# Projection slices spread through an RWKV-7 stage: the next head group's r, k, v inside the present group's inversion and chain, and the attention's first five projections between the steps of the samples' RWKV

## The chip, the core and the metric

The kernel runs on one core of one Trainium2 chip. The metric is the device time of one execution in microseconds (us), lower is better. The core has five engines that run side by side and meet at semaphores: TensorE (PE, matmuls; PEld is its weight load), VectorE (DVE), ScalarE (ACT), GpSimd (POOL) and SyncE (SP, which here only starts transfers). TensorE's clock is granted at one of two levels, 1.2 and 2.4 GHz; the profile gives it as 0.5 and 1.0.

## What is computed

One inference step of one decoder layer for 512 prompt tokens and 8 samples of 8 tokens (576 token columns in all), float32:

```python
x = x + 0.5 * SwiGLU(RMSNorm(x))                      # FFN 1
h = RMSNorm(x); P = h @ w_in                          # 1024 -> 4608 q,k,v | 1792 RWKV | 2048 gates
A = dilated sliding-window attention, 3 groups, QK-norm + ALiBi
u = p_shift + mu * (prev - p_shift)                   # token shift, gives r, k, v and the lora inputs
S = S * w_t - sk * (kk_t * a_t) + v_t * k_t ; o_t = S r_t     # RWKV-7 state, per head
o_rwkv = (layernorm(o) * gain + bias + bonus) * g
x = x + w_out( sigmoid(gA) * (A @ wa) + sigmoid(gR) * (R @ wr) )
x = x + 0.5 * SwiGLU(RMSNorm(x))                      # FFN 2
```

## The kernel before

**Units and slices.** Every projection is made in units: one unit is 128 output columns of a weight, over all 576 tokens, in three passes (high part of the weight by high and low part of the activation, low part by high part), each over eight tiles of the contraction. `unit_slice` (L333) issues one tile of the three passes, six matmuls of 128x128 by 288 columns: a slice. A unit is eight slices (KD = 8). Its weights come by one SP transfer into `w_raw` (`load_unit`, L309), are rounded by ACT into `w_hi` (`split_hi`, L315), and POOL subtracts to get `w_lo` (`split_lo`, L320). There are two buffers of each (even and odd units): a buffer's next weights are split after the unit before has been consumed, and the low part is what `unit_wait` on PE asks for, with the evacuation of the unit's PSUM banks. Units have a fixed order over the whole kernel, written out by hand on all engines and in the list `mids` on the host.

**Stages.** FFN 1; the prompt's RWKV (`rwkv_pe`, `rwkv_act`, `rwkv_dve`); a barrier; the samples' RWKV (`rwsam_*`); the output norm and gate of both (`rwout_*`); a barrier; attention (`att_*`); merge; FFN 2. A barrier is an order of PE, ACT and DVE alone (`barrier`, L351).

**The prompt's RWKV.** Two units for the lora inputs, then four head groups `ct` (two heads each). A head group starts with three units r, k, v for itself, each made at one go (`unit`); ACT copies each out of PSUM (`take`, L926), keeps the last token of each sequence (L929) and splits the weights two units on; DVE mixes it with the token before (`mix`, L1036 to L1041). Then come the lora matmuls (L722), the norm of kk (L730), transposes (L739), the bonus (L746), two products and five levels of a blockwise triangular inversion (L774; DVE's part L1104 to L1133, ACT's L989 and L995), three products, MV, XTK and W1 (L837, L845, L853), the transition matrices (L862), a chain of eight chunk states (L881, DVE L1156), and the output (L909, L916; DVE `UU` L1162; ACT L1014). Between these steps PE runs `fill(n)`: n slices of the head group's four gate units, 32 slices in all, whose results ACT stores to memory (`gate_out`, L954 and L957). `FILL` (line 83) says how many slices stand where. On ACT and DVE two head groups are one body of a loop of two.

**The samples' RWKV and the output.** Steps of 8 to 64 small matmuls with one DVE or ACT operation between them, no projection at all: transposes L1201, inversion L1183, the states (L1233 and L1248, 64x64 by 8 columns), the state updates (`SPREAD`, L1256 and L1257; DVE L1348), then per head group mean, variance and gate (L1375, L1383, L1390) with nine DVE operations (L1427 to L1440).

**Attention.** Four head groups with nine units each. The last four units of a head group are its own; the first five (AHEAD = 5) are made as slices in the head group before, and those of the first head group at one go at the start of the stage (`fill(AHEAD * KD, 0)`, 40 slices), with ACT's copies in front of everything else it does there. SP issues the mask and the weights of units 4 to 6 after barrier 3.

Of the kernel before, what the change touches and what calls it, by code (L numbers as in the profile page):

```python
# [23 lines left out]
ALU = mybir.AluOpType  # L24
# [7 lines left out]
NT = SEQ + NS  # L32
# [50 lines left out]
FILL = {"norm": 5, "tokens": (10, 1, 0, 0), "bonus": 0, "level": (1, 1, 1, 1, 0), "mv": 2, "xk": 2, "chunk": (1, 1, 1, 1, 1, 1, 1, 1)}  # L83
# [103 lines left out]
def build(nc, t):  # L187
# [11 lines left out]
    with ctx:  # L199
# [37 lines left out]
        beside_x.close()  # L237
        with ExitStack() as c:
# [7 lines left out]
            FM = sb(c, "fm", [128, 5, NT])  # L246
            KA, BH, KH, RH, UV = (FM[:, i] for i in range(5))
            TOK = sb(c, "tok", [128, 4, 4, 128])
            MV, W1 = sb(c, "mv", [128, 4, 128]), sb(c, "w1", [128, 4, 128])
            XK, UU = sb(c, "xk", [128, 512]), sb(c, "uu", [128, 4, 128])  # L250
            ST, XTK, GG = sb(c, "st", [128, NCH + 1, DH]), sb(c, "xtk", [128, 4, 128]), sb(c, "gg", [128, 2, 4, 128])
# [7 lines left out]
        with ExitStack() as c:  # L259
            QKV = sb(c, "qkv", [128, 3, 3, NT])  # L260
# [418 lines left out]
        def rw_units(i):  # L679

            return [(P_CT + 7 * i[0] + (7 * i[1] + n) // 2, (7 * i[1] + n) % 2, n) for n in range(3)]

        def gate_units(i):

            return [(P_CT + 7 * i[0] + (7 * i[1] + n) // 2, (7 * i[1] + n) % 2) for n in range(3, 7)]
# [7 lines left out]
        def rwkv_pe(pe):  # L693
            unit(pe, P_RW, 0, ready=("h_ready", 8, 0))
            unit(pe, P_RW, 1)
            pe.wait_ge(sem("lora_in_ready"), 2)
            for cc in range(2):
                for c2 in range(2):
                    ct = 2 * cc + c2
                    for P, q, n in rw_units((cc, c2)):  # L700
                        unit(pe, P, q)
                    filled = 0

                    def fill(slices):

                        nonlocal filled
                        for _ in range(slices):
                            P, q = gate_units((cc, c2))[filled // KD]
                            k = filled % KD
                            if k == 0:  # L710
                                unit_wait(pe, P, q)
                            last = unit_slice(q, h_hi, h_lo, k, k, KD, 2 * q)
                            if k == KD - 1:
                                last.then_inc(unit_done, 1)
                            filled += 1


# [8 lines left out]
                    fill(FILL["norm"])  # L726
# [1590 lines left out]
```

## Time and profile before

| | us |
|---|---|
| median of three runs (lowest, highest) | 1984.37 (1977.75, 1984.44) |
| the profiled execution, its own time | 1983.89 |
| its span, first to last instruction | 1982.1 |
| PE busy in the span | 1829.9 |
| DVE, ACT, POOL busy | 759.3, 627.3, 530.8 |
| prompt's RWKV, from its third unit to its last matmul | 492.7 to 906.9 |
| samples' RWKV and output, with both barriers | 906.9 to 1027.9 |
| the attention's first five units | 1027.9 to 1061.5 |

Times in a view are counted from the span's start. Busy time of PE is the union of its matmuls' durations, which overlap; the time of a run of like matmuls is read from start to start. In a row of a timeline the bracket gives the idle time ahead of it and what ended it.

### The profile page before, as it was taken

The page shows a single profiled execution, that of the slowest core. Times are in us where ns is not written, and L with a number is a line of the kernel's source. Part 1 is how long each engine was busy: PE and PEld are TensorE (multiplying, and loading weights), DVE is VectorE, ACT ScalarE, POOL GpSimd, SP SyncE. Part 2 cuts the span into 40 slices and gives each one's busy share as a digit, 9 for nine tenths or more (in the row PEclk, how much of TensorE's full clock was granted, in tenths as well). Part 3 has the DMA queues.
Part 4 walks back from the last instruction along what each step waited for, and adds up shares of the span by engine and source line. Part 5 has one row for each costly group of instructions (what it writes and reads, how often), then busy time and mean ns, then how long its engine had stood idle before and what let it go on. Part 6 is the DMA issues. An engine that isn't in the chain of part 4 may idle for free.

```text
span 1982.1 us, 41842 instructions
## 1 busy us (share of the span) xinstructions
PE 1829.9 (92%) x17032; PEld 1724.1 (87%) x17032; DVE 759.3 (38%) x1120; ACT 627.3 (32%) x828; POOL 530.8 (27%) x206
## 2 busy tenths in 40 slices
PE   7999999995898999887869999999899999999998
PEld 6999999994788888876549898988699999999998
DVE  4332033215535444452353454535456533113320
ACT  4332122223414141312024343434343433123321
POOL 2443344431203030300002121212033344334432
PEclk9999999998999999997569999999799999999999
DMA  4334333423404040411005444444453333333342
GB/s 152 118 116 138 103 114 119 135 96 111 157 29 144 25 175 30 152 40 68 17 25 182 163 161 163 168 160 168 178 192 106 117 126 116 128 112 122 113 143 110
DMA packets 52167, 237.47 MB, mean 120 GB/s; under 512 B 6992, under 2 KB 7632, under 8 KB 50512
## 3 DMA queue, kind: packets, MB, share of 16 engines
q1 hardware_dynamic: 44176, 219.40, 32.3%
q10 hardware_dynamic: 7872, 16.37, 2.2%
q8 instruction: 89, 1.46, 0.3%
q14 instruction: 30, 0.25, 0.0%
HBM read 217.98 MB, written 71.76 MB: 146 GB/s over the span
## 4 chain that ended last, share of the span: by engine, by line
issue 82%; POOL 13%; PE 4%; POOLq 1%; ACT 0%; ACTq 0%
POOL w_lo L320 13%; PE ps L333 4%; POOLq L627 0%; POOLq L319 0%; POOLq L2131 0%; POOLq L630 0%; ACT w_hi L315 0%; POOLq L320 0%; POOLq L626 0%; ACTq L314 0%; POOLq L2301 0%
## 5 line engine op out<-in xcount | busy, mean ns | idle before, releaser
L320 POOL TENSOR_TENSOR w_lo<-w_raw,w_hi 128x1024 fp32r<-128x1024 f32 (+1 forms) x202 | 530.6, 2627 | 1429.6 <-ACT w_hi L315 1429.6
L333 PE MATMUL ps<-h_hi,w_hi 128*128 128x288 f32 x2464 | 552.1, 306 | 40.6 <-POOL w_lo L320 14.0
L333 PE MATMUL ps<-h_lo,w_hi 128*128 128x288 f32 x2464 | 531.3, 298 | 0.0
L333 PE MATMUL ps<-h_hi,w_lo 128*128 128x288 f32 x2464 | 531.1, 297 | 0.0
L333 PEld LDWEIGHTS ps<-h_hi,w_hi 128*128 128x128 f32 x2464 | 400.0, 191 | 60.9 <-POOL w_lo L320 16.3
L333 PEld LDWEIGHTS ps<-h_lo,w_hi 128*128 128x128 f32 x2464 | 401.2, 191 | 0.0
L333 PEld LDWEIGHTS ps<-h_hi,w_lo 128*128 128x128 f32 x2464 | 400.4, 191 | 0.0
L315 ACT ACTIVATE w_hi<-w_raw 128x1024 fp32r<-128x1024 f32 (+1 forms) x204 | 226.3, 1109 | 432.8 <-PE ps L333 415.5
L333 PE MATMUL ps<-g_hi,w_hi 128*128 128x288 f32 x704 | 151.5, 297 | 0.1
L333 PE MATMUL ps<-g_lo,w_hi 128*128 128x288 f32 x704 | 151.3, 297 | 0.0
L333 PE MATMUL ps<-g_hi,w_lo 128*128 128x288 f32 x704 | 151.2, 297 | 0.0
L589 DVE SCALAR_TENSOR_TENSOR gt<-ps,nry 128x576 f32<-128x576 f32 x44 | 33.4, 758 | 241.1 <-PE ps L333 241.1
L333 PEld LDWEIGHTS ps<-g_hi,w_hi 128*128 128x128 f32 x704 | 113.7, 189 | 1.1 <-POOL w_lo L320 1.1
L602 DVE SCALAR_TENSOR_TENSOR x<-ps,x 128x576 f32 (+1 forms) x32 | 24.2, 758 | 235.9 <-PE ps L333 235.9
L333 PEld LDWEIGHTS ps<-g_hi,w_lo 128*128 128x128 f32 x704 | 113.8, 189 | 0.0
L333 PEld LDWEIGHTS ps<-g_lo,w_hi 128*128 128x128 f32 x704 | 113.8, 189 | 0.0
L595 DVE TENSOR_TENSOR g_lo<-gt,g_hi 128x576 f32 x44 | 87.4, 1986 | 42.4 <-ACT g_hi L555 42.4
L550 ACT ACTIVATE sg<-sg 128x576 f32<-128x576 f32 x44 | 30.2, 686 | 158.2 <-DVE sg L586 158.2
L586 DVE SCALAR_TENSOR_TENSOR sg<-ps,nry 128x576 f32<-128x576 f32 x44 | 33.4, 758 | 88.2 <-PE ps L333 87.5
L1734 ACT ACTIVATE qkv<-ps 128x576 f32<-128x576 f32 x36 | 23.4, 651 | 127.1 <-PE ps L333 127.1
L774 PE MATMUL ps<-xt,lmask 64*64 64x64 f32 x640 | 29.6, 237 | 14.7 <-DVE lmask L1110 8.2
L550 ACT ACT_TABLE_LOAD x30 | 38.5, 1283 | 13.0 <-issue 13.0
(365 smaller groups left out, 2023.1 us busy)
## 6 DMA issues: line engine op xcount, KB each, us to landing
w_raw<-in_w SPq DMA_DIRECT2D x172, 512.0 KB, 3.5
w_raw<-in_w SPq DMA_DIRECT2D x32, 704.0 KB, 4.0
kv<-in_kc SPq DMA_DIRECT2D x32, 576.0 KB, 5.9
kv<-in_vc SPq DMA_DIRECT2D x32, 576.0 KB, 7.3
cache_out<-in_cache SPq DMA_DIRECT2D x28, 576.0 KB
gates<-gate_out ACTq DMA_DIRECT2D x16, 288.0 KB, 2.1
gate_in<-gates SPq DMA_DIRECT2D x8, 576.0 KB, 5.0
cache_out<-in_cache SPq DMA_DIRECT2D x8, 480.0 KB
```

Source lines behind the costliest of these rows:

```text
L315: nc.scalar.activation(w_hi[par_][:, 0:words], w_raw[par_][:, 0:words], ACT.Copy).then_inc(hi_done, 1)
L320: nc.gpsimd.tensor_tensor(w_lo[par_][:, 0:words], w_raw[par_][:, 0:words], w_hi[par_][:, 0:words].bitcast(F32), ALU.subtract).then_inc(lo_ ...
L333: last = nc.tensor.matmul(ps[:, b + c, 0:HC], w[par_][:, wk], a[:, k, c * HC:(c + 1) * HC], start=(first and k == 0), stop=(end and k == n ...
L550: nc.scalar.activation(sg[:, :], sg[:, :], ACT.Silu).then_inc(sem("silu_done"), 1)
L586: nc.vector.scalar_tensor_tensor(two(sg[:, :]), bank2(0), back(0), two(nry[:, :]), ALU.mult, ALU.mult).then_inc(evac[0], 1)
L589: nc.vector.scalar_tensor_tensor(two(gt[:, :]), bank2(2), back(0), two(nry[:, :]), ALU.mult, ALU.mult).then_inc(evac[1], 1)
L595: nc.vector.tensor_tensor(g_lo[:, j, :], gt[:, :], g_hi[:, j, :].bitcast(F32), ALU.subtract).then_inc(sem("g_ready"), 1)
L602: nc.vector.scalar_tensor_tensor(two(x[:, k, :]), bank2(2 * q), 0.5, two(x[:, k, :]), ALU.mult, ALU.add)\
L774: last = nc.tensor.matmul(ps[rows_of(e), 4 + (2 * n + h) % 4, 64 * T:64 * T + 64], lhs(T, e), rhs(T, e), start=True, stop=True)
L1734: nc.scalar.activation(two(QKV[:, g, kind, :]), bank2(b), ACT.Copy).then_inc(evac[q], 1)
```

## The change

What it does, in parts:

1. **Order of units** in the prompt's RWKV (`RW_UNITS`, and `mids` on the host): lora 2, r, k, v of head group 0, then for each `ct` gates 0 to 2, r, k, v of `ct + 1`, gate 3.
2. **PE**: only the five first units are made at one go. The other 25 (200 slices) come through `fill`, with counts that add up to 56 a head group (53 up to the end of the first one, 35 left for the last one). New places: ahead of the products, at the fifth level, and in the tail.
3. **ACT**: `gate_out` and `take` stand at new places in the queue: gate 3 of the group before after the square of kk, gates 0 and 1 ahead of the copies of the transposes, gate 2 ahead of LR, r after the levels, k after W1, v ahead of the copy of the output. The waits for stored gates at a head group's end are gone. PR is chosen by the count of mixes.
4. **DVE**: the mixes of `ct + 1` stand after the products and at the end of the chain. The loops of ACT and DVE are written out. DVE waits for `x_kept` before the first mixes of r, k, v.
5. **Memory**: QKV of the attention and part of the RWKV's tiles (FM, MV, UU, XTK, ST) lie over the same space outside the stages' own, so that the attention's raw projections can be written during the samples' RWKV.
6. **Samples' RWKV and output**: 40 slices of the attention's first five units in 16 fills of 2, 3 or 6, PSUM banks 0 and 1 for them; the stage's own banks are moved up, the gate of the output has one pair of banks in place of two (so that it waits for the DVE's last operation of the head group before), ACT takes the raw projections and splits the next weights between its steps. Variance goes before the next mean on PE.
7. **Output on DVE**: three operations (L1436, L1437, L1438) become two.
8. **Attention**: its 40 slices at the start are gone, with ACT's five copies and splits. One memset (L1840) is gone, the scaled masks (L1888) are made after `spread` in each head group, SP loads weights 4 to 7 ahead of barrier 3 and the masks behind the first three key transfers.

```diff
-FILL = {"norm": 5, "tokens": (10, 1, 0, 0), "bonus": 0, "level": (1, 1, 1, 1, 0), "mv": 2, "xk": 2, "chunk": (1, 1, 1, 1, 1, 1, 1, 1)}
+FILL = {"norm": 9, "tokens": (11, 1, 1, 0), "bonus": 2, "products": 3, "level": (3, 2, 2, 2, 2), "mv": 3, "xk": 2,
+        "chunk": (1, 1, 1, 1, 1, 1, 1, 1), "tail": (3, 2)}
+RW_UNITS = [("lora", 0, 0), ("lora", 0, 1)] + [("mix", 0, n) for n in range(3)]
+for _ct in range(CT):
+    RW_UNITS += [("gate", _ct, n) for n in range(3)] + [("mix", _ct + 1, n) for n in range(3) if _ct + 1 < CT] + [("gate", _ct, 3)]
...
             for cc in range(2):
                 for c2 in range(2):
                     ct = 2 * cc + c2
-                    for P, q, n in rw_units((cc, c2)):
-                        unit(pe, P, q)
...
-                    fill(FILL["norm"])
+                    fill(FILL["norm"] if ct else KD - 2)
...
+                    fill(FILL["products"])
...
+                    fill(FILL["tail"][0])
...
+                    fill(FILL["tail"][1])
...
                     act.wait_ge(sem("kkr_ready"), ct + 1)
                     nc.scalar.activation(TT[:, :], KA, ACT.Square).then_inc(sem("kk_sq"), 1)
                     act.drain()
+                    if ct:
+                        gate_out(ct - 1, 3)
...
-                    gate_out(0)
+                    gate_out(ct, 0)
+                    gate_out(ct, 1)
                     for a in range(2):
...
-                    gate_out(1)
...
+                    gate_out(ct, 2)
...
+                    if ct + 1 < CT:
+                        take("mix", ct + 1, 0)
+                    else:
+                        gate_out(ct, 3)
                     act.wait_ge(sem("mv_done"), ct + 1)
...
+                    if ct + 1 < CT:
+                        take("mix", ct + 1, 1)
                     for half in range(2):
                         act.wait_ge(sem("xk_done"), 2 * ct + half + 1)
...
-                    gate_out(2)
...
+                    if ct + 1 < CT:
+                        take("mix", ct + 1, 2)
                     act.wait_ge(sem("o_done"), ct + 1)
...
-                    gate_out(3)
-                    for q in range(2):
-                        act.wait_ge(sem("gate_stored%d" % q), 16 * (2 * ct + 2))
-                    act.wait_ge(sem("wkvp_stored"), 16 * (ct + 1))
...
-            scores(0, 0, 1)
-            scores(2, 1, 0)
+            scores(2, 0, 1)
+            fill(2)
+            pe.wait_ge(sem("s_tok_a"), 2)
+            scores(4, 1, 0)
+            fill(6)
             pe.wait_ge(sem("s_inv"), 1)
             pe.wait_ge(sem("s_tok_d"), 2)
             heads(6, mm(SLM), mm(SXT))
+            fill(2)
             pe.wait_ge(sem("s_act"), 2)
             heads(7, mm(SZZ), mm(SXX))
             heads(4, mm(SXX), mm(SZZ))
+            fill(3)
             pe.wait_ge(sem("s_inv"), 2)
             heads(6, mm(SLM), mm(SXT))
+            fill(3)
...
                 nc.tensor.matmul(o, TOS[1][:, hc(ct, h)], SPREAD[h][0], start=True, stop=False)
                 nc.tensor.matmul(o, TOS[2][:, hc(ct, h)], SPREAD[h][1], start=False, stop=True).then_inc(sem("s_dstate"), 1)
+                if h:
+                    fill(2)
...
             mean(0)
             gate(0)
-            for ct in range(CT):
+            mean(1)
+            fill(2)
+            var(0)
+            fill(2)
+            for ct in range(1, CT):
+                var(ct)
                 if ct + 1 < CT:
                     mean(ct + 1)
-                var(ct)
-                if ct + 1 < CT:
-                    gate(ct + 1)
+                    fill(2)
+                gate(ct)
...
-                own(V.tensor_tensor(FT[:, :], FO[ct % 2][:, :], FY[ct % 2][:, :], ALU.mult))
-                own(V.tensor_scalar(FT[:, :], FT[:, :], P1("lng", ct), P1("lnb", ct), ALU.mult, ALU.add))
-                own(V.tensor_tensor(FT[:, :], FT[:, :], BN[:, ct, :], ALU.add))
+                own(V.scalar_tensor_tensor(FT[:, :], FO[ct % 2][:, :], P1("lng", ct), FY[ct % 2][:, :], ALU.mult, ALU.mult))
+                own(V.scalar_tensor_tensor(FT[:, :], FT[:, :], P1("lnb", ct), BN[:, ct, :], ALU.add, ALU.add))
...
-                if hp == 0:
-                    fill(AHEAD * KD, 0)
-                    filled = 0
                 own_slices(0, 0, 2)
                 norm(0)
```

## Rows read from the trace of the kernel before

**Rows 1.** The page, busy time of PE and its weight loads.

```profile
PE 1829.9 (92%) x17032; PEld 1724.1 (87%) x17032; DVE 759.3 (38%) x1120; ACT 627.3 (32%) x828; POOL 530.8 (27%) x206
```

**Rows 2.** Busy time by stage: length, then each engine, then clock and DMA.

```profile
492.70:595.90 103.20, 92.69 (x1259) 84.98 (x1259) 45.86 (x87) 29.01 (x47) 14.96 (x6) 0.96 0.26 94
...
801.10:906.90 105.80, 93.36 (x1259) 85.37 (x1258) 49.52 (x87) 29.92 (x49) 17.81 (x7) 0.95 0.24 85
906.90:912.60 5.70, 0.00 (x0) 0.00 (x0) 0.00 (x0) 2.19 (x3) 2.34 (x1) 0.74 0.13 52
912.60:939.30 26.70, 19.63 (x224) 17.91 (x225) 9.64 (x15) 4.82 (x7) 0.00 (x0) 0.61 0.24 82
939.30:951.70 12.40, 11.18 (x136) 10.56 (x133) 0.68 (x1) 0.97 (x2) 0.00 (x0) 0.54 0.00 1
951.70:966.90 15.20, 15.14 (x160) 15.04 (x160) 0.00 (x0) 0.00 (x0) 0.00 (x0) 0.50 0.01 1
966.90:989.50 22.60, 20.20 (x32) 5.91 (x32) 14.84 (x23) 0.38 (x1) 0.00 (x0) 0.50 0.09 35
989.50:1027.90 38.40, 19.35 (x48) 11.93 (x48) 24.91 (x34) 8.82 (x13) 0.00 (x0) 0.63 0.02 8
1027.90:1061.50 33.60, 33.60 (x236) 33.60 (x237) 5.27 (x8) 8.11 (x9) 9.57 (x4) 0.93 0.25 78
```

**Rows 3.** PE's waits from 492 to 907: us in total, times, longest.

```profile
PE ps L739 <- DVE fm L1065: 8.4, 4, 2.2
PE ps L774 <- DVE lmask L1110: 8.2, 8, 1.5
...
PE ps L333 <- POOL w_lo L320: 5.0, 2, 3.1
...
PE ps L739 <- DVE fm L1072: 0.6, 3, 0.2
```

**Rows 4.** PE's waits from 907 to 1028.

```profile
PE ps L1383 <- DVE tmp L366: 5.5, 3, 2.7
PE ps L1390 <- DVE o_rw L1440: 4.8, 2, 2.5
PE ps L1183 <- DVE lmask L1312: 3.4, 1, 3.4
...
PE ps L1183 <- DVE lmask L1318: 2.0, 1, 2.0
...
PE ps L1183 <- ACT zz L1262: 1.4, 2, 0.7
...
PE ps L1183 <- ACT xx L1262: 0.2, 1, 0.2
```

**Rows 5.** Timeline of PE: start, duration; slices and heads at either clock.

```profile
493.87 0.68 PE L333 MATMUL ps<-h_hi,w_lo 128*128 128x288 f32 x2
...
495.31 0.68 PE L333 MATMUL ps<-h_hi,w_lo 128*128 128x288 f32 x2
...
920.90 1.96 PE L1183 MATMUL ps<-xt,lmask 64*64 64x64 f32 x16 [3.43 <-DVE lmask L1312]
...
938.35 1.14 PE L1183 MATMUL ps<-xx,xt 64*64 64x64 f32 x16 [0.21 <-ACT xx L1262]
...
1058.06 0.43 PE L333 MATMUL ps<-h_hi,w_hi 128*128 128x288 f32 x2
...
1058.87 0.42 PE L333 MATMUL ps<-h_hi,w_hi 128*128 128x288 f32 x2
```

**Rows 6.** DVE's L1063 and L1061 (one form), from source and timeline.

```profile
L1063 DVE SCALAR_TENSOR_TENSOR tmp<-fm,sw x4: 2811/2820/2821, 527.8 to 839.3; 128x576 f32<-128x576 f32 x4
...
833.67 0.76 DVE L1061 SCALAR_TENSOR_TENSOR u_k<-fm,u_k 128x576 f32<-128x576 f32 x1
```

**Rows 7.** PE in the state updates: length, busy, clock, DMA.

```profile
972.00:988.00 16.00, 16.00 (x28) 0.50 0.08 33
```

**Rows 8.** Timeline of DVE, the operation that falls away.

```profile
1002.58 0.58 DVE L1437 TENSOR_SCALAR tmp<-tmp,par 128x576 f32<-128x576 f32 x1
```

More of the change, by code:

```diff
@@ L677, in build, with rw_unit @@
         IN_BANK = (7, 4)
[L679 to L685, printed above, removed]
+        def rw_unit(kind, ct, n):
+            i = RW_UNITS.index((kind, ct, n))
+            return P_RW + i // 2, i % 2
         def rows_of(h):
@@ L696, in rwkv_pe, with fill @@
             pe.wait_ge(sem("lora_in_ready"), 2)
+            for n in range(3):
+                unit(pe, *rw_unit("mix", 0, n))
+            filled = 0
+            def fill(slices):
+                nonlocal filled
+                for _ in range(slices):
+                    i, k = 5 + filled // KD, filled % KD
+                    if i == len(RW_UNITS):
+                        return
+                    P, q = P_RW + i // 2, i % 2
+                    if k == 0:
+                        unit_wait(pe, P, q)
+                    last = unit_slice(q, h_hi, h_lo, k, k, KD, 2 * q)
+                    if k == KD - 1:
+                        last.then_inc(unit_done, 1)
+                    filled += 1
             for cc in range(2):
@@ L1178, in mc, with ahead_pe, fill, rwsam_pe @@
             return slice(256 * h + 64 * ct, 256 * h + 64 * ct + 64)
-        def rwsam_pe(pe):
+        def ahead_pe(pe, of, state):
+            def fill(slices):
+                if of == CT:
+                    return
+                for _ in range(slices):
+                    n, k = state[0] // KD, state[0] % KD
+                    P, q = at_unit(of, n)
+                    if k == 0:
+                        unit_wait(pe, P, q)
+                        if of or n:
+                            Pb, qb = at_unit(of, n - 1)
+                            pe.wait_ge(evac[qb], Pb + 1)
+                    last = unit_slice(q, h_hi, h_lo, k, k, KD, FBANK)
+                    if k == KD - 1:
+                        last.then_inc(unit_done, 1)
+                    state[0] += 1
+            return fill
+        def rwsam_pe(pe, fill):
             def heads(bank, lhs, rhs, where=mc):
@@ L1712, in att_pe @@
                     fill(5)
-                    assert hp + 1 == CT or filled == AHEAD * KD
+                    assert hp + 1 == CT or state[0] == AHEAD * KD
         def att_act(act):
@@ L1750, in guess @@
                     rsqrt_act(own, bank2(NORM_BANK[i]), ary[i % 2], 3)
-                if hp == 0:
-                    for n in range(AHEAD):
-                        take(0, n)
                 square_of(0)
@@ L1898, in att_dve @@
                     spread()
+                    if hp == 0:
+                        dve.wait_ge(sem("mask_loaded"), 16)
+                    for h in range(2):
+                        V.tensor_scalar(MSC[:, h, :], MSK[:, 0:512], P1("slp", 2 * hp + h), None, ALU.mult)
+                    dve.drain()
                     apply(4)
@@ L2067, in _ @@
             barrier(pe, 2)
-            rwsam_pe(pe)
-            rwout_pe(pe)
+            first = [0]
+            fill = ahead_pe(pe, 0, first)
+            rwsam_pe(pe, fill)
+            rwout_pe(pe, fill)
+            assert first[0] == AHEAD * KD
             barrier(pe, 3)
@@ L2097, in _ @@
             act.wait_ge(sem("shift_stored"), 16)
+            for i in range(2):
+                act.wait_ge(sem("gate_stored%d" % i), 16 * 2 * CT)
             act.wait_ge(sem("x_kept"), 16)
```

227 lines of the change are left out of this document (115 added, 112 removed).

## The prediction

> **What bounds the kernel now.** I read the page first: PE is busy for 1829.9 of 1982.1 us [rows 1]. That is a union of overlapping matmuls, so at best 152 us of the span are open, and only PE's order of work can give time back. Next I cut the span at the code's stages [rows 2]. The reader should see three kinds of stretch. A head group of the prompt's RWKV takes 103 to 106 us, of which PE is busy for some 93, near full clock. From 912.6 to 1027.9 there is no projection: PE's clock is 0.50 to 0.63 and between the barriers only the small steps run. From 1027.9 to 1061.5 it is the reverse: PE works without a gap, DVE and ACT are nearly idle. Last I asked for PE's waits in the first two kinds [rows 3, 4]: each is a wait of a few us at most for one DVE, ACT or POOL operation. PE's order bounds all of it; the waits are the only room.
>
> **Price of a slice.** Two like passes of neighbouring slices start 495.31 - 493.87 = 1.44 us apart at the half clock and 1058.87 - 1058.06 = 0.81 at the full one [rows 5]; over a whole unit the full pitch is 0.80. So a slice is 0.80 or 1.44 us. The change keeps their number. What it can gain is waits filled, and clock; what it can lose is new waits.
>
> **A, the prompt's RWKV (492.7 to 906.9).** PE's waits there, without the one ahead of 492.75 that stays, are twelve rows of the view with a sum of 42.9 us [rows 3]. Twenty-four slices of each of head groups 1 to 3, now made at one go, move into the steps, and fills grow exactly where the waits are: 9 for 5 ahead of the norm, 13 for 11 in the transposes, 5 new ones ahead of bonus and products (4.0 us, more than the longest of these waits), 11 for 4 in the levels. Waits with no slices ahead of them (L845, L746, and three of the transposes' short ones) make 5.3 us. So 37.6 can go; 5.0 of it are the stands for `w_lo` [rows 3], where split and unit followed each other too closely at the old head group's start.
>
> Three things come back. First, the last head group has 35 slices left in place of 56: from the fifth level on its steps run bare. At most 0.80 is uncovered at each of the eleven or so places, 8.8 in all, at least nothing; I take 5, as a chain step's own DVE latency is about half of what its slice covered. Second, ACT: five copies that PE waits for (TOK, LR, MV, XK, the output) now stand behind a copy and a split of about 2 us. I followed each: for MV and the output the unit is ready early and the step itself is slower than ACT; for TOK and LR the margins are under 1 us. Third, POOL beside DVE. L1063, with two inputs in SBUF, takes 2.82 us in all four head groups, L1061 of the same form 0.76 [rows 6]; each L1063 starts while POOL is in a `w_lo`. So an exposed meeting costs 2.06 us. Before, POOL made none of a head group's splits between the first products and the chain's second half; now three to four of the seven splits fall there, onto the DVE operations after the first products, on the first mixes and, by `gate_out(ct, 1)` moved ahead, on BH and KH. Bounds: none exposed, 0; one at each of the five places in four head groups, 20 x 2.06 = 41. The nearest rows are the two margins under 1 us, so I take 2.65 us a head group, 10.6: one meeting and half a microsecond of ACT. A = -(37.6 - 5 - 10.6) = **-22**, from -32.6 to +8.4.
>
> The GPSIMD Engine Reference of the Trainium skill (Specifications) says that GpSimd shares its SBUF interfaces with VectorE and that they contend when a VectorE instruction has two SBUF inputs. The trace agrees (2.82 against 0.76), and this speaks against the change: taken for every split that now falls into the inversion it would give the upper bound, not the value taken.
>
> Unrolled loops on ACT and DVE, and the wait for `x_kept`, I cost at nothing: PE's unit 3 covers the latter; if that transfer came later, head group 0 would start late by as much.
>
> **B, the end of the stage.** The 5.70 us between the last matmul and the first of the samples hold only ACT's last copies, gate 3's store and a wait for it, with PE at nothing [rows 2]. The store moves ahead; the state's own store remains. Between -4 and 0, I take **-2**.
>
> **C, samples' RWKV and output (912.6 to 1027.9): 40 slices, 31.9 us at the full clock, 57.6 at the half one.** Step by step:
> - 912.6 to 939.3, 20 slices, 15.9 us (28.8). They stand ahead of waits of 3.4 + 2.0 + 1.4 + 0.2 = 7.0 [rows 4]. Eight heads' matmuls take 1.96 us at the half clock and 1.14 near the full one [rows 5]; with dense slices between I expect the full clock for most, and five such steps gain 4: +5. Bounds +4 and +21.8.
> - 939.3 to 966.9: 4 slices. Their own clock will be low (64x8 matmuls run at 0.50 to 0.54 through 27 us with PE busy [rows 2]), 5.8 us less 1.3 of waits, less 1 for the first steps at a better clock: +3.5. Bounds +1, +4.5.
> - 966.9 to 989.5, the state updates: 8 slices. PE is busy 20.20 of 22.60 at 0.50, DVE 14.84 [rows 2]. At the half clock PE is the bound and 8 x 1.44 = 11.5 add up, less 1.6 that cover the last update's DVE part: +10. At the full clock PE's part halves and DVE is the bound: 0. I take +4.
> - 989.5 to 1027.9: 8 slices, ahead of waits of 5.5 + 4.8 = 10.3 [rows 4]. DVE sets the pace (24.91 busy, each step following on its own or ACT's last). It loses L1437's 0.58 four times [rows 8], -2.4 with the issue. The first fill stands ahead of `var(0)`, which PE would reach at once: +1.5. The gate's single bank pair makes its matmuls wait, but DVE needs them only some 6 us later. -1; bounds -2.4 and +2.
>
> C = +5 + 3.5 + 4 - 1 = +11.5, taken as **+12**, from +3 to +38.
>
> **D, attention.** The 33.6 us of 1027.9 to 1061.5 are 40 slices and nothing beside them that something waits for [rows 2]: ACT's five copies and splits go with them. 33.6 - 40 x 0.80 = 1.7 is the start at the half clock, which the next units now pay. **-31.9**. What is late next: the first norm waits for ACT's squares, which now start behind a table load, some 2 us, as PE's two slices do; the key transfers start with the stage, about where they stood against the unit they precede; the masks come behind three of them, used only after `spread`. I price these at 0. The scaled masks moved on DVE: 0, PE has slices beside them.
>
> **Sum.** -22 - 2 + 12 - 31.9 = -43.9. The profiled execution took 1983.89, 0.5 under the median of the runs, so both stand for the same level: 1983.9 - 43.9 = **1940**.
>
> **Rivals.**
> 1. *All of it at the full clock.* If the slices lift the clock through the samples' stage, C is +3 and the time 1931. For it: stretches dense with slices run at 0.93 to 0.96 [rows 2]. Against it: 16 us of state updates with PE busy for 16.00 ran at 0.50 [rows 7]. The page TensorE: Matmul & The Clock Gate of the Trainium skill (Part 1) has the clock rise with sustained PE busyness; the trace disagrees here, as these matmuls were busy throughout and the clock stayed low. By the page's rule the present clock would be no guide, and this rival would be the forecast. Chance 0.15.
> 2. *The half clock stays through the samples' stage.* C is +38, the time 1966. For it: every row from 940 to 989.5. Against: slices at 1.44 us each make PE denser than anything in it now. Chance 0.10.
> 3. *The prompt's RWKV gains nothing*: waits filled come back behind ACT and POOL. A = 0, 1962. For it: 2.82 against 0.76 and the thin margins. Against: the waits are many and short. Chance 0.12.
> 4. *Slower: the ACT queue.* One mechanism: in the prompt's RWKV, ACT stands for the last slice of a unit while the copy that PE needs queues behind it, so that PE makes slices in place of steps and then stands. Five places in four head groups; without A the change gives -21.9, so at 1.1 us each they eat it, and at 1.6 (+0.5%) decide. The most is about 2 us of copy and split and 2.06 of POOL, 4.1 us each: 82, or 2044. Against it: three of the places have slack of several us. Chance 0.04.
> 5. *No change*, by half of rivals 3 and 2 together with a late weight transfer: within 0.5%, 0.05.
>
> The forecast keeps 0.54. Its own range is 1932 to 1954. The range for 8 in 10 takes in rival 1 and 3 and most of the way to 2: 1922 to 1964. 0.5% is 10 us, about what a measurement of this kernel can tell from no change. Faster by more: 0.54 + 0.15 + 0.10 + 0.12 = 0.91; within: 0.05; slower: 0.04.
>
> **What would show it.** After the change head groups 1 and 2 should take about 97 us, the last one under 90, the first about 112 (it has 75 slices in place of 56). PE's waits there should add up to less than 20, those for `w_lo` to none. Between the last prompt matmul and the attention's own first unit there should be some 131 us, with all 40 slices inside, and granted clocks well above 0.6 before the 64x8 matmuls. The attention should begin with `own_slices`. DVE operations of two SBUF inputs that take 2 us and more inside the inversion would prove the POOL term; PE waits for `zz`, `lraw` or `tok` the ACT one. The prediction is wrong if the samples' stage grows by more than 25 us, or if slices and steps in a head group add up to the old 104.

## Result and the profile after

The changed kernel takes 1916.67 us (median of 4 runs, 1911.29 to 1919.15) against 1982.28 (4 runs, 1977.75 to 1984.44) of the kernel before, in turns on the same chip: ratio 0.967, 95% interval 0.964 to 0.970. It is faster, and by more than forecast: 1916.67 lies under the range of 1922 to 1964. Its profiled execution took 1916.84, with a span of 1915.0, so 67.1 less than the one of before.

I cut both spans at the same instructions. The boundaries are: PE's third unit of the prompt's RWKV, ACT's last copy of the output, the first transposes of the samples, the attention's first unit, and the merge's first matmul.

| us | before | after | difference | predicted |
|---|---|---|---|---|
| start to the prompt's third unit | 492.8 | 490.7 | -2.1 | 0 |
| A, prompt's RWKV | 414.2 | 382.8 | -31.4 | -22 |
| B, its end to the samples' first step | 5.6 | 1.3 | -4.3 | -2 |
| C, samples' RWKV and output | 115.3 | 114.2 | -1.1 | +12 |
| D, attention | 403.7 | 376.3 | -27.4 | -31.9 |
| merge and FFN 2 | 550.5 | 549.7 | -0.8 | 0 |
| sum | 1982.1 | 1915.0 | -67.1 | -43.9 |

Over all profiles below, the first row lies between 490.7 and 493.8 whatever the kernel, so its 2.1 is no part of the change. A and C are the two terms that missed, by 9.4 and 13.1.

The page's first line after the change, against [rows 1]:

```profile
PE 1796.3 (94%) x17032; PEld 1703.2 (89%) x17032; DVE 777.8 (41%) x1115; ACT 623.4 (33%) x825; POOL 534.4 (28%) x206
```

The same 17032 matmuls took 33.6 us less. The slices are as many as before, so the shorter union of busy time comes from matmuls that ran faster (the mean clock over the span rose from 0.951 to 0.969) or that overlap more; how much of it is the clock is worked out for the prompt's stage under E6. Busy time by stage, with the columns of [rows 2]: head groups 0, 2 and 3, the end, then the samples' stage up to the 64x8 matmuls, these up to the second group of them, up to the state updates, the state updates, the output.

```profile
490.70:603.80 113.10, 106.12 (x1373) 99.49 (x1373) 54.45 (x97) 32.25 (x54) 22.84 (x9) 0.97 0.33 118
698.80:792.70 93.90, 88.80 (x1259) 82.84 (x1259) 49.61 (x88) 29.92 (x49) 18.23 (x7) 0.98 0.35 127
792.70:873.50 80.80, 73.46 (x1145) 67.56 (x1144) 44.67 (x78) 25.79 (x43) 13.44 (x5) 0.98 0.24 79
873.50:874.80 1.30, 0.03 (x1) 0.03 (x2) 0.00 (x0) 0.57 (x2) 0.00 (x0) 1.00 0.00 0
874.80:904.30 29.50, 29.50 (x345) 27.63 (x346) 9.65 (x15) 8.24 (x11) 4.74 (x2) 1.00 0.23 75
904.30:918.70 14.40, 14.40 (x159) 14.05 (x156) 0.68 (x1) 0.97 (x2) 0.00 (x0) 0.64 0.01 1
918.70:931.80 13.10, 10.75 (x161) 10.64 (x160) 1.70 (x3) 2.09 (x3) 2.34 (x1) 0.71 0.13 41
931.80:953.00 21.20, 21.14 (x80) 11.73 (x80) 14.53 (x23) 0.00 (x0) 0.00 (x0) 0.78 0.10 38
953.00:989.00 36.00, 21.45 (x99) 16.04 (x97) 23.65 (x28) 12.27 (x17) 4.73 (x2) 0.86 0.07 23
```

The reader should compare the clocks with [rows 2]. The first 20 slices of the samples' stage and the steps between them run at 1.00 where the steps alone ran at 0.61: 29.5 us now hold 15.9 us of slices and take 2.8 us more than the 26.7 without (4.2 more than the 25.3 of E1 below, which has the change without these slices). Further on 0.64, 0.71, 0.78 and 0.86 stand where 0.50 to 0.63 stood.

The same in two rows of PE's timeline, after: the 64x8 matmuls of the second group, 16 of a head in 1.05 us (before 1.82).

```profile
918.99 1.05 PE L1298 MATMUL ps<-sv,tok 64*64 64x8 f32 x16
920.16 0.99 PE L1298 MATMUL ps<-sv,tok 64*64 64x8 f32 x15
```

PE's waits in the prompt's stage after, the largest of it (the 8.7 us stand ahead of the stage, as before):

```profile
PE ps L776 <- DVE lmask L1125: 12.2, 8, 1.6
PE ps L338 <- ACT u_g L958: 8.7, 1, 8.7
PE ps L741 <- DVE qkv L1087: 4.4, 3, 1.5
PE ps L741 <- DVE qkv L1083: 2.2, 1, 2.2
PE ps L848 <- DVE lmask L1157: 2.0, 4, 0.5
...
PE ps L338 <- POOL w_lo L325: 0.8, 1, 0.8
```

The stands ahead of the norm (tmp) and the bonus are gone, and of those for `w_lo` 0.8 is left; the first level's wait for `lmask` (8.2 in [rows 3]) has grown to 12.2. The sum is 23.4 us, against 42.9 before.

### The profile page after: what moved, and what is told of

Same layout as the page of the kernel before. It is cut to its first block, busy times and chain, and to the rows that moved or that the text cites. A ratio compares the mean times of both kernels' runs of the same rounds, so it can differ in the third digit from the quotient of the medians.

```text
span 1915.0 us, 41445 instructions
## 1 busy us (share of the span) xinstructions
PE 1796.3 (94%) x17032; PEld 1703.2 (89%) x17032; DVE 777.8 (41%) x1115; ACT 623.4 (33%) x825; POOL 534.4 (28%) x206
## 4 chain that ended last, share of the span: by engine, by line
issue 81%; POOL 14%; PE 4%; POOLq 1%; ACT 0%; ACTq 0%
POOL w_lo L325 14%; PE ps L338 4%; POOLq L632 0%; POOLq L324 0%; POOLq L2183 0%; POOLq L635 0%; ACT w_hi L320 0%; POOLq L325 0%; POOLq L631 0%; ACTq L319 0%; POOLq L2360 0%
## 5 line engine op out<-in xcount | busy, mean ns | idle before, releaser
L1004 ACT ACTIVATE zz<-ps 128x256 f32<-128x256 f32 x40 | 15.4, 384 | 91.9 <-PE ps L776 90.7
```

The source lines that it names most:

```text
L1004: nc.scalar.activation(ZZ[h][:, 0:256], ps[:, 4 + (2 * n + h) % 4, 0:256], ACT.Copy).then_inc(sem("mat_a%d" % h), 1)
```

## Experiments

Two theories went into them. Theory 1: slices between small steps lift TensorE's clock, so the steps themselves get shorter; that would explain C, and the part of A that filled waits can't. Theory 2, the rival: the slices cost what they cost, and the gain comes from other parts (the shorter output on DVE, the new order, fewer waits).

All profiles, cut as above:

| us | A: head groups 0, 1, 2, 3 | A | C | state updates to first mean | D |
|---|---|---|---|---|---|
| before | 103.3, 104.1, 101.1, 105.8 | 414.2 | 115.3 | 21.8 | 403.7 |
| changed | 113.1, 95.0, 93.9, 80.7 | 382.8 | 114.2 | 21.2 | 376.3 |
| changed, again | 114.6, 92.6, 96.1, 83.2 | 386.5 | 122.4 | 28.4 | 372.9 |
| E1 prompt only | 114.8, 92.6, 94.4, 84.1 | 385.8 | 112.2 | 21.8 | 406.2 |
| E2 masks back | 115.0, 92.6, 93.4, 83.0 | 384.0 | 114.3 | 21.1 | 369.7 |
| E3 no late slices | 115.0, 92.5, 94.2, 81.9 | 383.6 | 118.1 | 21.1 | 371.6 |
| E4 gate 2 later | 112.7, 90.5, 90.5, 78.7 | 372.3 | 115.8 | 20.6 | 375.1 |
| E5 gate 1 later | 111.6, 92.2, 92.2, 80.4 | 376.5 | 116.1 | 20.4 | 374.1 |
| E6 all moves | 107.5, 88.8, 88.8, 76.9 | 361.9 | 114.2 | 21.1 | 369.7 |
| E6 again | 108.0, 88.8, 88.8, 77.0 | 362.5 | 116.1 | 20.4 | 367.7 |
| E7 three operations | 114.9, 92.6, 94.2, 81.8 | 383.4 | 125.9 | 28.1 | 374.3 |
| E8 slices ahead | 108.0, 88.8, 88.8, 77.0 | 362.5 | 114.4 | 16.8 | 367.7 |

### E1: the prompt's part alone

All 40 slices go back to the start of the attention, with ACT's copies and splits; everything else stays as changed.

```diff
-            rwsam_pe(pe, fill)
-            rwout_pe(pe, fill)
+            rwsam_pe(pe, lambda slices: None)
+            rwout_pe(pe, lambda slices: None)
...
+                if hp == 0:
+                    for n in range(AHEAD):
+                        P, q = at_unit(0, n)
+                        unit_wait(pe, P, q)
+                        for k in range(KD):
+                            last = unit_slice(q, h_hi, h_lo, k, k, KD, 2 * (n % 2))
+                        last.then_inc(unit_done, 1)
                 own_slices(0, 0, 2)
...
```

> The changed kernel with the 40 slices of the samples' RWKV and output taken out again and made at one go at the start of the attention, as before, with ACT's copies; the rest of the change stays. Theory 1 (the slices keep TensorE at 2.4 GHz in a stage that otherwise runs at 1.2, so they cost nothing): from the first transposes to the attention 111 to 113 us (115.3 before, less 2.4 for DVE's operation), granted clock again about 0.5 in the 64x8 matmuls and the state updates, attention's start again 33.6; in all the time rises by about 31 us over the changed kernel, to 1948. Rival (the recorded sum: slices cost 12 us net there): it rises by 20, to 1937.

Measured 1948.73 us (4 runs, 1948.25 to 1953.43) against 1982.04, ratio 0.984 (0.982 to 0.987), as theory 1 had it. So about half of the gain is the prompt's part and half the slices in the samples' stage. Windows of E1, cut like those of after (transposes, first 64x8 group, up to the state updates, state updates, output, and the five units at one go):

```profile
878.30:903.60 25.30, 18.19 (x224) 17.02 (x225) 9.65 (x15) 4.81 (x7) 0.00 (x0) 0.66 0.13 45
903.60:915.80 12.20, 10.99 (x135) 10.36 (x133) 0.68 (x1) 0.97 (x2) 0.00 (x0) 0.55 0.01 1
915.80:933.40 17.60, 15.16 (x161) 15.07 (x161) 1.71 (x3) 0.38 (x1) 0.00 (x0) 0.50 0.00 1
933.40:955.20 21.80, 20.20 (x33) 5.95 (x33) 14.51 (x22) 0.00 (x0) 0.00 (x0) 0.50 0.09 36
955.20:990.50 35.30, 19.39 (x49) 12.20 (x49) 21.69 (x28) 8.84 (x13) 0.00 (x0) 0.74 0.02 8
990.50:1024.00 33.50, 33.50 (x241) 33.50 (x242) 2.63 (x5) 8.08 (x9) 9.57 (x4) 0.95 0.18 55
```

Without slices the clock of the 64x8 matmuls and the updates is 0.50 to 0.55 again. The stage takes 112.2 us, so 40 slices, 31.9 us at the full clock, cost 2.0 in the first profile of the changed kernel (114.2) and give back 33.5 at the attention's start. By part, the changed kernel less E1: up to the 64x8 matmuls 29.5 - 25.3 = +4.2; up to the state updates 27.5 - 29.8 = -2.3; state updates -0.6; output +0.7. The other parts of the change in this stage are worth 115.3 - 112.2 = 3.1, of which 1.4 fall before the 64x8 matmuls (26.7 against 25.3, no slices in either) and 1.5 in the output. Theory 2 has those 3.1, theory 1 the rest. The 2.0 are those of one profile; the changed kernel's second profile, below, gives another figure.

### E3: no slices between the first 64x8 matmuls and the state updates

The last two fills of 2 are moved ahead of the first 64x8 matmuls, so that their number stays.

```diff
-            fill(2)
+            fill(4)
             pe.wait_ge(sem("s_dve"), 2)
...
-            fill(2)
+            fill(4)
             pe.wait_ge(sem("s_act"), 4)
...
-            fill(2)
             pe.wait_ge(sem("s_act"), 6)
...
-            fill(2)
             pe.wait_ge(sem("s_dve"), 6)
```

> The changed kernel with the two fills of 2 slices between the two groups of 64x8 matmuls moved ahead of the first group. Theory 1 (the slices matter for the clock of what follows them): the second group, 13.1 us, runs at 1.2 GHz again and takes about 15 us from its first matmul, the state updates start at 1.2 GHz, and the stage from the transposes to the attention grows by 2 to 4 us. Rival (the slices only fill waits of 1.3 us): the stage changes by less than 1.5 us, as the four slices are cheaper at the full clock.

Measured 1917.55 us (one run). The windows of E3 on both sides of the first 64x8 group, and up to the state updates:

```profile
878.60:911.50 32.90, 32.85 (x369) 31.00 (x370) 9.65 (x15) 8.25 (x11) 4.75 (x2) 1.00 0.21 67
911.50:922.20 10.70, 9.46 (x136) 8.84 (x134) 0.68 (x1) 2.66 (x4) 0.00 (x0) 0.65 0.01 2
922.20:939.70 17.50, 15.13 (x160) 15.03 (x160) 1.71 (x3) 0.41 (x2) 2.34 (x1) 0.50 0.10 31
```

The last row is the second 64x8 group: 17.5 us at 0.50 for the same steps that take 13.1 at 0.71 with four slices ahead of them. Where the four slices stand is nearly all one for themselves: 3.4 us more in the first part (32.9 against 29.5), 3.7 less in the second (10.7 against 14.4). But the steps behind lose 4.4, and the stage is 3.9 us longer. That is theory 1 at one place: the slices' own time is earned back by the steps behind them.

The 4.4 depend on the profile that E3 is held against. The three profiles without slices ahead of this group (before, E1, E3) all have 17.5 at 0.50. The eight with the changed kernel's fills have 13.0 to 13.2 in four (changed, changed again, E2, E6) and 15.3 to 15.7 in the other four. The row of E6's second profile:

```profile
899.90:915.40 15.50, 13.10 (x162) 13.00 (x161) 1.71 (x3) 2.09 (x3) 2.34 (x1) 0.58 0.11 35
```

So the four slices are worth 1.8 to 4.5 us behind them; the sign is certain, the size is not. The same holds for the stage: E3's 118.1 is 2.0 to 3.9 above the six profiles with these fills and fast updates (114.2 to 116.1).

### The changed kernel again, and E7: three operations in the output

The changed kernel, unedited; and the changed kernel with the three DVE operations of before:

```diff
-                own(V.scalar_tensor_tensor(FT[:, :], FO[ct % 2][:, :], P1("lng", ct), FY[ct % 2][:, :], ALU.mult, ALU.mult))
-                own(V.scalar_tensor_tensor(FT[:, :], FT[:, :], P1("lnb", ct), BN[:, ct, :], ALU.add, ALU.add))
+                own(V.tensor_tensor(FT[:, :], FO[ct % 2][:, :], FY[ct % 2][:, :], ALU.mult))
+                own(V.tensor_scalar(FT[:, :], FT[:, :], P1("lng", ct), P1("lnb", ct), ALU.mult, ALU.add))
+                own(V.tensor_tensor(FT[:, :], FT[:, :], BN[:, ct, :], ALU.add))
```

> The changed kernel once more, on the same chip as the version with three moves, for comparison: 1917, and within 3 us of it in each stage of the profile.

> The changed kernel with the output's three DVE operations per head group in place of two. Theory 1 (DVE sets the pace from the last state update to the attention): this stretch grows by 2.4 us, four times 0.6. Rival (ACT's guess or PE's new order sets it): by less than 1 us.

Measured: 1922.70 us for the changed kernel (5 runs, 1917.94 to 1927.83; ratio 0.969, 0.966 to 0.972), 1927.66 for E7 (one run). I had expected every stage of the changed kernel within 3 us of its first profile; A is 3.7 off and C 8.2. In both kernels the stretch from the first state update to the first mean takes 28 us where it takes 20 to 21 in the other profiles with these fills. The window of the changed kernel's second profile there:

```profile
936.60:965.00 28.40, 28.40 (x81) 15.55 (x82) 14.52 (x22) 0.00 (x0) 0.00 (x0) 0.50 0.07 28
```

PE is busy for all of 28.40 us, at 0.50; in the first profile the same instructions take 21.2 at 0.78 (above). The code is the same, so the clock there comes out one way or the other from run to run, and the 7.2 us between them are most of the 8.2 by which C differs between the two profiles. A single profile of this kernel therefore settles C to no better than that: by this one the 40 slices cost 122.4 - 112.2 = 10.2 us, not 2.0. E7 is best read against the second profile, which had the slow updates too: from the first mean to the attention it takes 38.2 us against 37.0, so the saved operation is worth 1.2 us, not the 2.4 that I took; E1, with no slices in either kernel, gives 36.8 - 35.3 = 1.5 for this part of the change. E7 is one run, and against the first profile (36.0) it would be 2.2, so the size is open between 1.2 and 2.2. The groups of DVE in the output show why, first of E7 (L1521 of the even head groups), then of the first profile after:

```profile
L1521 DVE TENSOR_TENSOR tmp<-exp_p,cumx 128x576 f32<-128x576 f32 x2 | 3.5, 1771 | 0.1
L1523 DVE TENSOR_TENSOR tmp<-tmp,bonus 128x576 f32<-128x576 f32 x4 | 3.0, 759 | 0.1
...
L1522 DVE TENSOR_SCALAR tmp<-tmp,par 128x576 f32<-128x576 f32 x4 | 2.3, 578 | 0.1
```

```profile
L1521 DVE SCALAR_TENSOR_TENSOR tmp<-exp_p,par,cumx 128x576 f32<-128x576 f32 x2 | 3.6, 1800 | 0.1
L1522 DVE SCALAR_TENSOR_TENSOR tmp<-tmp,par,bonus 128x576 f32<-128x576 f32 x4 | 3.3, 819 | 0.1
```

One operation of 0.578 is gone, and two of 0.759 have become 0.819: DVE has 0.46 less to do per head group, 1.8 in all. L1521 has a mean of 1800 because one of its two instances takes 2.78 beside a POOL split: head group 2's meets the split of the attention's weights, in E7 as well.

### E4 and E5: take POOL's splits off two DVE operations

What did A lose? The timeline of head group 2 after the change, first DVE, then POOL:

```profile
719.59 0.76 DVE L1085 TENSOR_TENSOR qkv<-u_k,exp_m 128x576 f32<-128x576 f32 x1
720.44 2.76 DVE L1087 TENSOR_TENSOR qkv<-u_r,exp_p 128x576 f32<-128x576 f32 x1
...
731.41 1.82 DVE L1121 TENSOR_TENSOR xx<-lraw,con 128x256 f32<-128x256 f32 x1 [0.82 <-ACT lraw L998]
733.26 0.42 DVE L1122 TENSOR_TENSOR xx<-xx,con 128x256 f32<-128x256 f32 x1
```

```profile
719.80 2.79 POOL L325 TENSOR_TENSOR w_lo<-w_raw,w_hi 128x1024 fp32r<-128x1024 f32 x1 [3.34 <-ACT w_hi L320]
730.56 2.38 POOL L325 TENSOR_TENSOR w_lo<-w_raw,w_hi 128x1024 fp32r<-128x1024 f32 x1 [7.97 <-ACT w_hi L320]
```

RH (L1087, the product whose transposes PE makes last) and the first product of the inversion behind ACT's copy (L1121) each start inside a split and end 0.61 and 0.29 us behind its end: 2.76 for 0.76 and 1.82 for 0.42. L1121 is also 0.82 late behind ACT's `lraw`, which stood behind the split's first half. Both operations stand on PE's path. So E4 makes gate 2's copy and split one step later on ACT, behind the first level's copy, and E5 gate 1's behind the copies of TOK:

```diff
-                    gate_out(ct, 2)
                     act.wait_ge(sem("x_kept"), 16)
...
+                        if lv == 0:
+                            gate_out(ct, 2)
```

```diff
                     gate_out(ct, 0)
-                    gate_out(ct, 1)
...
                         act.drain()
+                    gate_out(ct, 1)
```

> The changed kernel with ACT's copy of gate 2, its split and store moved behind the first level's copies in each head group. Theory 1 (ACT's queue, 0.8 us, and POOL's split beside the first DVE operation of the inversion, 1.4 us, hold up its start): the waits for lmask fall from 12.2 us to about 5, that DVE operation takes 0.43 us in place of up to 1.82, each head group gets 2 us shorter, the prompt's RWKV some 8 us. Rival (the two waits are the DVE chain itself, POOL only moves on to the next level): less than 2 us in all, with DVE operations of over 1.5 us in the levels.

> The changed kernel with ACT's copy of gate 1, its split and store moved behind the copies of the first two transposes, where it stood before. Theory 1 (POOL's split beside RH costs the last transposes their 1.47 us): RH takes 0.76 us in all head groups in place of 2.76, PE's wait for it goes, the prompt's RWKV gets 4 to 5 us shorter. Rival (PE is late elsewhere, as the copies come no earlier to it): less than 1.5 us.

Measured 1908.1 and 1911.15 us (one run each). Six profiles with A as changed have a mean of 384.4 (382.8 to 386.5); E4 has 372.3 and E5 376.5, so -12.1 and -7.9, and both lie clear of the six. The operation's row (count: shortest, median, longest in ns), in E4:

```profile
L1122 DVE TENSOR_TENSOR xx<-lraw,con x8: 424/425/426, 545.9 to 819.5; 128x256 f32<-128x256 f32 x8
```

and in the changed kernel, where it is 1822 at the most:

```profile
L1121 DVE TENSOR_TENSOR xx<-lraw,con x8: 425/1122/1822, 542.4 to 828.9; 128x256 f32<-128x256 f32 x8
```

PE's wait for the operations behind it, in E4:

```profile
PE ps L776 <- DVE lmask L1126: 4.0, 4, 1.0
```

The wait of 12.2 is 4.0, less than the 8.2 of before. In E5 RH takes 759 ns at the most and the waits at L741, 4.4 and 2.2 in the changed kernel, are 0.2. The mechanism is shown by E5: taking the meeting away takes the wait away. E4 takes away the meeting and ACT's 0.82 us together, so how the 8.2 divide between them is not shown. The GPSIMD Engine Reference of the Trainium skill (Specifications) has GpSimd and VectorE contend for the SBUF interfaces when a VectorE instruction reads two operands there; by that rule, the trace agrees.

But the stage gains more than the wait: 12.1 for 8.2, 7.9 for 6.4. The windows from the first product of head group 1 to the end of its inversion show where to look: before, changed, the changed kernel's second profile, E6.

```profile
642.00:671.00 29.00, 24.89 (x571) 22.72 (x572) 15.31 (x37) 4.60 (x12) 0.52 (x1) 0.88 0.15 44
```

```profile
633.75:666.80 33.05, 29.93 (x614) 27.95 (x614) 16.64 (x37) 7.63 (x17) 2.39 (x1) 0.90 0.09 30
```

```profile
636.30:666.90 30.60, 27.47 (x613) 25.38 (x613) 16.60 (x37) 7.58 (x17) 2.39 (x1) 1.00 0.10 32
```

```profile
629.20:657.50 28.30, 27.21 (x612) 25.19 (x612) 15.04 (x37) 7.41 (x17) 2.38 (x1) 1.00 0.21 71
```

In the first profile the clock falls within this stretch (0.90), in the second, with the same stands, it does not (1.00). So one head group decides nothing; all of them together do. I counted the stretch from the first product to the last matmul of the inversion in every head group. The seven profiles with the stands ahead of the first level (changed twice, E1, E2, E3, E5, E7) have 28 such stretches: the clock fell to 0.89 to 0.95 in 20 and stayed at 1.00 in 8. The four without (E4, E6 twice, E8) have 16, all at 1.00. In head groups 0 to 2 the stretch takes 28.0 us without the stands, 30.1 with them at 1.00, and 31.4 to 32.6 where the clock fell (three stretches, 30.9, 31.9 and 33.6, are left out: PE stood a further 0.5 to 1.6 us in them for no cause that the trace names). E4 and E5 tell the stands apart: E4 still has those at the transposes, and all four of its stretches are at 1.00; E5 has only those ahead of the first level, and all four are at 0.94 to 0.95. So a stand here costs its length, 2.1 us a head group, and in most cases 1.3 to 2.5 us more by the clock.

### E2 and E6: the masks at their old place, and all moves together

E2 puts DVE's scaled masks, for all head groups but the first, back behind the state's products at the end of the head group before. E6 is E2, E4 and E5 together.

```diff
+                    if hp:
+                        for h in range(2):
+                            V.tensor_scalar(MSC[:, h, :], MSK[:, 0:512], P1("slp", 2 * hp + h), None, ALU.mult)
+                        dve.drain()
                     v_place(1)
...
```

> The changed kernel with the scaled masks (two DVE operations of 0.88 us) made ahead of v_place again in head groups 1 to 3. Theory 1 (they now stand on the path from the norms to the first scores, 1.8 us each head group): the time falls by 5 us, to 1911, the attention from 376 to 371 us, and PE's waits for nmx and vsam shrink. Rival (hidden, as in the recorded prediction; the attention's extra comes from its start): no change, the attention stays at 376.

> The changed kernel with three moves together: masks back, gate 2 late, gate 1 late. Theory 1: the three add up, 5 + 8 + 5 = 18 us, to about 1899. Rival (each frees only what the next wait takes): 1908 to 1917.

> The version with all three moves once more, on the same chip as the version with two slices ahead of the state updates. Its time should be that measured for it before, 1896.6, within 6 us; head groups 361 to 363 us together, state updates 21 or 28 us.

Measured: E2 1914.96 us (1913.01 to 1916.72; ratio 0.966, 0.964 to 0.968), E6 1896.64 (5 runs, 1890.61 to 1899.27; ratio 0.956, 0.953 to 0.959) and once more 1893.28 (ratio 0.955, 0.953 to 0.957). By D, six profiles with the masks behind `spread` (without E1, which has five units more in D) have a mean of 374.1 (371.6 to 376.3), the four with them back 368.7 (367.7 to 369.7): the move that I priced at 0 costs 5.4 us. Half of it is idle time of PE in this stage, 18.9 to 20.9 us in the six and 16.9 to 17.5 in the four; the other half is busy time, where the two sets overlap, so its cause is not shown. PE's waits for the scores' scaling in the attention, changed, then E2:

```profile
PE ps L1661 <- DVE nmx L1956: 3.2, 5, 0.7
```

```profile
PE ps L1661 <- DVE nmx L1960: 1.3, 2, 0.7
```

Of the whole time E2 alone resolves nothing (1914.96 beside 1916.67 and 1922.70). E6 does: it beats both kernels, 20.0 and 23.4 us under the changed one's 1916.67, and 26.1 under the 1922.70 measured beside it. A is 361.9 and 362.5, so 22 us under 384.4, where E4 and E5 alone add up to 20.0. The prompt's stage as a whole, in windows of before, changed and E6:

```profile
492.70:906.90 414.20, 370.82 (x5032) 339.65 (x5032) 189.94 (x348) 120.10 (x195) 67.59 (x27) 0.96 0.26 93
```

```profile
490.70:873.50 382.80, 358.31 (x5032) 333.81 (x5032) 198.33 (x348) 117.88 (x195) 72.74 (x28) 0.97 0.29 103
```

```profile
493.50:855.40 361.90, 352.04 (x5032) 328.22 (x5032) 184.83 (x348) 117.77 (x194) 71.13 (x28) 0.99 0.31 109
```

The same 5032 matmuls. PE's idle time (length less busy) goes 43.4, 24.5, 9.9; its busy time 370.8, 358.3, 352.0, with the clock at 0.96, 0.97, 0.99. To three digits the clock is 0.958, 0.973 and 0.991. The stage's length times the share not granted, 17.4, 10.3 and 3.3 us, is an upper estimate of what the half clock cost, so the clock explains at most 7.1 of the 12.5 us of busy time that the changed kernel saves, and at most 14.1 of the 18.8 of E6. What the other 5 us or so are is not shown.

### E8: slices in the one wait that is left in the samples' stage

E6 with two slices ahead of the state updates, where PE waits 2.4 us for the first spread, and none behind the last update.

```diff
+            fill(2)
             for ct, h in HEADS:
...
-                if h:
+                if h and ct + 1 < CT:
                     fill(2)
```

> The version with all three moves (gate copies 1 and 2 later, scaled masks at their old place) and, in the samples' RWKV, two slices ahead of the state updates, where TensorE stands for some 2.4 us, and none after the last update. The slices stay 40. In the profiles so far the 64x64 matmuls by 512 columns of the updates ran either with the clock rising after the second update (about 21 us from the first of them to the first mean) or at half throughout (about 28 us) with the same code. If the clock hangs on how closely slices stand ahead of the updates, two slices in the wait bring the stretch to 18 to 20 us in the profile and to no 28; slices in the wait cost nothing, the two after the last update fall away: stage at 112 to 113 us, time 1893 to 1896, 0 to 4 under the version without. If it is chance that does not depend on the order, the time is that of the version without within 2 us, and the profile can show 28 again. If DVE sets the updates at the full clock, the stretch can't fall below about 17.

Measured 1895.78 us (5 runs, 1890.95 to 1901.81; ratio 0.957, 0.955 to 0.959), beside 1893.28 of E6 on the same chip: no gain. Windows of E8 from the second 64x8 group on:

```profile
899.80:916.00 16.20, 16.20 (x173) 15.90 (x172) 2.36 (x5) 2.09 (x3) 2.34 (x1) 0.58 0.11 33
916.00:932.80 16.80, 15.20 (x69) 8.34 (x69) 13.87 (x22) 1.52 (x2) 0.00 (x0) 1.00 0.12 48
932.80:970.30 37.50, 22.64 (x97) 16.91 (x97) 23.65 (x28) 10.74 (x16) 4.69 (x2) 0.82 0.07 22
```

The updates ran at 1.00 in 16.8 us, the least of all profiles, as theory 1 has it, though with six slices among them in place of eight; with the group ahead, which holds the other two, it is 33.0 us against 34.3 and 35.9 in E6. I had expected the stage at 112 to 113. It is 114.4, within those of E6 (114.2 and 116.1): at the full clock DVE is the bound (13.87 busy of 16.8, and PE waits 1.6 for its last update), and the output is longer by 1.2 to 1.6. The expected 1893 to 1896 us holds by its number, but not as a gain on E6. Whether this order rules out the 28 us case, one profile can't say.

## Why the prediction missed

**Direction and mechanism** held: waits filled in A, the attention's five units gone, B shorter. The size missed by 23.2 us (-67.1 for -43.9): -13.1 from C, -9.4 from A, -2.3 from B, -2.1 ahead of the change, -0.8 behind it, +4.5 from D. Half of that is the luck of one execution: the changed kernel's second profile has a span of 1926.0, 56.1 under before, with -4.9 from C and -5.8 from A.

**The step that failed is C's choice of the clock between 939.3 and 989.5, "+3.5" and "I take +4".** Measured by part against before, first profile: up to the 64x8 matmuls +2.8 (taken +5); up to the state updates -2.4 (14.4 + 13.1 against 12.4 + 17.5; taken +3.5, bounds +1 and +4.5, the sign was wrong); state updates -0.6 (taken +4); output -0.9 (taken -1). In the second part I priced slices at the half clock with 1 us for better steps. The slices gave the 64x8 matmuls behind them a higher clock, and E3 shows what that is worth at this place, 1.8 to 4.5 us; over the profiles with the changed kernel's fills this part came to between -2.5 and +0.2. For the updates I took a value between the two clocks, and the runs gave one or the other: -1.4 to -0.6 in seven profiles with the fills where they are, +6.3 and +6.6 in two. The first part's +5 was nearly right: against E1 the slices cost +4.2, and the other 1.4 came from the rest of the change, which I had at nothing there. I read the rows at 0.50 as a property of those steps. For the 64x8 matmuls they were a property of what ran ahead of them; for the updates only in eight profiles of ten.

**Rival 1** (all at the full clock, C +3) came nearest for C, at 0.15: C is -1.1 in the first profile and +7.1 in the second. Its row against, [rows 7], 16 us busy at 0.50, was right as a row: the changed kernel again has 28.40 of 28.40 busy at 0.50. The page TensorE: Matmul & The Clock Gate of the Trainium skill (Part 1), which has the clock rise with sustained busyness, is borne out by the slices and not by this row.

**A, filled waits.** 37.6 were to go, 5 and 10.6 to come back, net 22 of idle time. In idle time: 43.4 - 9.9 = 33.5 go (E6), 24.5 - 9.9 = 14.6 come back through the two meetings, net 18.9. The 5 for the last head group's missing slices was somewhat high: as the table cuts it, this head group has 19 slices less than the one before (1145 matmuls for 1259), in E6 88.8 less 19 x 0.80 is 73.6, and it takes 76.9, so 3.3. The POOL term was right in kind, 4 short in size (14.6 for 10.6) and one operation off in place: I named BH and KH, it met RH, and BH's own factor in head group 0; the first operations after the products were right. **What my sum had no term for** is PE's busy time, -12.5 in the changed kernel and -18.8 in E6 for the same matmuls. With the 3.1 by which the idle time fell short of 22, those are the 9.4 that A missed by. At most 7.1 of the 12.5 is the clock (above); the rest stays open. I had the clock's part in view: [rows 2] have 0.95 for a head group, and I wrote "near full clock" and went on.

**What I said would show it.** Head groups 1 and 2 took 95.0 and 93.9 (about 97), the first 113.1 (112), the last 80.7 (under 90). PE's waits there came to 23.4, not under 20, and 0.8 was left for `w_lo`, not none. From the last prompt matmul to the attention's first unit it took 115.5, not 131. DVE operations of 2 us and more stood in RH, ahead of the inversion, and 1.82 inside it.

**B**: -4.3, just past its bound of -4; the 1.3 that stay are the barrier. **D**: the 33.6 are gone, and the masks, priced at 0 because "PE has slices beside them", cost 5.4 (E2). The rest of the attention is 1.4 shorter than before (370.1 to 368.7).

**Rivals 2 to 5**: the half clock did not stay (except in the updates of two profiles), the prompt's RWKV did gain, and ACT's queue cost its share only at one place, 0.82 us of `lraw`.

**Open**: what decides in a given run whether the clock rises in the state updates, and whether a stand makes it fall in the inversion. Of ten profiles of kernels with slices there, eight had 16.8 to 21.2 us and two had 28; no run here tells which condition tips it.

## What to carry to other kernels

Where small steps run at the half clock, dense matmuls put between them have two prices: their own time, and the time that they give back to every step behind them; here 31.9 us of slices cost 2.0 in one execution and 10.2 in another. Count the half-clock time of a stretch as room of its own beside its waits, also where the clock reads 0.95, and take more than one profile before you price it. And when work is spread through a stage, look where its side work (here POOL's subtraction) lands on the other engines: two copies moved down ACT's queue were worth 20 us of 384.

## What was not expected of the hardware

The same code at the same place ran 21.2 us at 0.78 and 28.4 us at 0.50, with PE busy throughout both. Small matmuls follow the clock as large ones do: 16 of 64x64 by 8 columns took 1.05 us behind slices and 1.82 without. Stands of 1.6 us and less ahead of the inversion's first level went with a fall of the clock behind them in 20 of 28 head groups, and without them it fell in none of 16. And a DVE operation that meets a POOL subtraction is not slowed in proportion: one of 128x256 ends 0.29 us behind the subtraction's end and one of 128x576 0.61, each about 0.14 less than it takes alone (0.42 and 0.76; it took 1.82 and 2.76). So nearly all its own time comes after the subtraction.
